# The order of one load queue in a two-block network: head pairs, gates and modulation weights

## The reference, cut to what matters

```python
proj = h @ w_in
(m_z, m_xbc, m_dt, b_qkv, c_qkv, c_f, d_q, d_kv, gate_logits) = jnp.split(proj, SPLIT_POINTS, axis=-1)
y_a = mamba2_branch(m_z, m_xbc, m_dt, ...)
y_b = moba_attention(heads(bq, N_HEADS), heads(bk, N_HEADS), heads(bv, N_HEADS), ...)
y_c = forgetting_attention(heads(cq, N_HEADS), heads(ck, N_HEADS), heads(cv, N_HEADS), ...)
y_d = sliding_window_attention(heads(d_q, N_HEADS), ...)
branch_out = jnp.einsum('bsiw,iwd->bsid', branches, w_branch)
gates = jax.nn.sigmoid(gate_logits.reshape(bsz, s_len, N_BRANCHES, D_MODEL))
return jnp.sum(gates * branch_out, axis=2) @ w_out
```

## Time and profile before

| | us |
|---|---|
| median of 3 runs | 1218.05 |
| the three runs | 1218.87, 1216.9, 1218.05 |
| the profiled execution | 1222.76 |
| its span, from the first to the last record | 1221.0 |
| TensorE busy in it | 1169.3 (96%) |
| VectorE busy | 496.0 (41%) |
| ScalarE busy | 215.0 (18%) |
| GpSimd busy | 79.7 (7%) |
| mean granted TensorE clock | 0.977 |
| moved from memory | 158.11 MB, 130 GB/s over the span |

### The profile page before, as it was taken

One profiled execution on the slowest core, in us unless ns is written; L12 is line 12 of the kernel. 1 busy time (PEld: TensorE's weight loads), 2 busy tenths in 40 slices (PEclk: granted clock), 3 DMA queues, 4 the chain that ended last, 5 costly groups with the idle time before them and its releaser, 6 DMA issues.

```text
span 1221.0 us, 19636 instructions
## 1 busy us (share of the span) xinstructions
PE 1169.3 (96%) x8368; PEld 958.6 (79%) x8368; DVE 496.0 (41%) x1232; ACT 215.0 (18%) x545; POOL 79.7 (7%) x119
## 2 busy tenths in 40 slices
PE   6999999999999999999998998999999999999997
PEld 5888888878787677777776876878778787877886
DVE  3343333424431210000004494657666665766332
ACT  3121121203100100000003321212122121213101
POOL 1100000000022000000001011010101101010000
PEclk8999999999999899999998999999999998999999
DMA  7426446371556233535343403031221404051230
GB/s 265 135 93 242 176 169 249 121 296 41 185 147 233 112 132 119 189 121 190 121 173 120 161 18 139 27 131 53 105 95 62 156 5 153 19 208 53 86 122 35
DMA packets 50570, 160.48 MB, mean 131 GB/s; under 512 B 5394, under 2 KB 10418, under 8 KB 50484
## 3 DMA queue, kind: packets, MB, share of 16 engines
q1 hardware_dynamic: 49764, 158.12, 36.5%
q10 hardware_dynamic: 720, 1.11, 0.3%
HBM read 158.11 MB, written 1.10 MB: 130 GB/s over the span
## 4 chain that ended last, share of the span: by engine, by line
PE 91%; DMA 4%; DVE 4%; ACT 0%; issue 0%; SPq 0%; DVEq 0%
PE bank L377 38%; PE bank L677 21%; PE bank L586 8%; PE bank L831 3%; DMA slots<-in_w_rwkv 2%; PE bank L985 2%; PE bank L509 2%; PE bank L818 2%; DVE arena L1657 1%; PE bank L712 1%; DMA slots<-in_w_heads 1%; PE bank L656 1%; PE bank L445 1%; PE bank L780 1%; PE bank L389 1%; PE bank L690 1%
## 5 line engine op out<-in xcount | busy, mean ns | idle before, releaser
L377 PE MATMUL bank<-hT,slots 128*128 128x256 f32 x1760 | 390.4, 382 | 5.9 <-DMA slots<-in_w_heads 3.7
L377 PEld LDWEIGHTS bank<-hT,slots 128*128 128x128 f32 x1760 | 335.3, 191 | 59.5 <-issue 10.3
L677 PE MATMUL bank<-hT,slots 128*128 128x256 f32 x1152 | 284.3, 396 | 17.5 <-DMA slots<-in_w_rwkv 16.3
L677 PEld LDWEIGHTS bank<-hT,slots 128*128 128x128 f32 x1152 | 217.5, 195 | 51.0 <-DMA slots<-in_w_rwkv 17.1
L1657 DVE SCALAR_TENSOR_TENSOR arena<-padA,par,arena 128x256 f32<-128x256 f32 x232 | 109.6, 530 | 0.0
L586 PE MATMUL bank<-slots,arena 128*128 128x512 f32 x240 | 105.0, 592 | 0.0
L377 PE MATMUL bank<-arena,slots 128*128 128x256 f32 x432 | 94.6, 381 | 0.0
L377 PEld LDWEIGHTS bank<-arena,slots 128*128 128x128 f32 x432 | 82.7, 191 | 11.5
L586 PEld LDWEIGHTS bank<-slots,arena 128*128 128x128 f32 x240 | 45.6, 190 | 52.3 <-issue 51.7
L1550 DVE SCALAR_TENSOR_TENSOR arena<-arena,bank 128x256 f32<-128x256 f32 x22 | 9.3, 422 | 134.9 <-ACT arena L1121 134.9
L1462 DVE SCALAR_TENSOR_TENSOR adaA<-arena,sc,adaA 128x1024 f32<-128x1024 f32 x24 | 30.7, 1283 | 78.2 <-DMA arena<-in_ada_w 78.0
(11 more groups left out here) (306 smaller groups left out, 1156.1 us busy)
## 6 DMA issues: line engine op xcount, KB each, us to landing
slots<-in_w_rwkv SPq DMA_DIRECT2D x72, 512.0 KB, 4.6
slots<-in_w_heads SPq DMA_DIRECT2D x68, 512.0 KB, 8.1
slots<-in_w_gu SPq DMA_DIRECT2D x44, 512.0 KB, 4.4
arena<-in_ada_w SPq DMA_DIRECT2D x24, 512.0 KB, 4.4
slots<-in_w_down SPq DMA_DIRECT2D x22, 512.0 KB, 3.8
slots<-in_w_br SPq DMA_DIRECT2D x32, 256.0 KB, 2.6
slots<-in_w_out SPq DMA_DIRECT2D x16, 512.0 KB, 5.4
slots<-in_w_y SPq DMA_DIRECT2D x16, 512.0 KB, 4.4
```

What stands on the lines that cost most here:

```text
L377: end = e.matmul(psum, w[:, k * P:(k + 1) * P], rhs[:, k, :], start=k == 0, stop=k == kt - 1)
L677: end = e.matmul(proj(w, q), slot[w][:, k * P:(k + 1) * P], hT[:, k, :], start=k == 0, stop=k == KT - 1)
```

## The change

Only SyncE's stream is changed, in `sp_heads`. No transfer is added or taken away, no wait names another step, and the streams of the four other engines stay as they are, instruction by instruction. What changes is the order of the requests within a pair i:

1. The nine head slices of pair i + 1 are asked for in the middle of pair i, behind gates 0 to 2 and modulation pieces 0 and 1, where before they stood at the start of pair i + 1, behind piece 5 of pair i.
2. The decay loads of pair i + 1 are asked for behind gate 4 of pair i, where before they stood behind slice CQ of pair i + 1.
3. Modulation pieces 0 and 1 stand behind gate 2 instead of gate 3, piece 2 stands ahead of gate 5, piece 3 ahead of gate 6; behind gate 7 only pieces 4 and 5 are left, where it was 3, 4 and 5.

```diff
+            def head_loads(i):
+                for n, before, step in ((BQ, "bc0", "qb"), (BK, "bc1", "kb"), (CQ, "dk0", "qc"), (CK, "dk1", "kc"), (DQ, "dv", "qd"),
+                                        (BV, "bc2", "vbc"), (CV, "bc3", "vbc"), (XS, None, "xs"), (ZS, None, "zs")):
                     if i:
-                        e.wait_ge(*dve.upto(f"mx.c11.{i - 1}"))
-                        e.wait_ge(*dve.upto(f"d11.{i - 1}"))
-                    else:
+                        e.wait_ge(*pe.upto(f"{step}.{i - 1}"))
+                    elif before:
+                        e.wait_ge(*pe.upto(before))
+                    load(e, n, a["w_heads"][i * NW + SLICE[n], :, :], f"w{n}.{i}")
...
+            if i == 0:
+                head_loads(0)
-            for j in range(4):
+            for j in range(3):
                 gate_load(j)
-            for n in range(3):
+            for n in range(2):
                 ada_load(n)
-            for j in range(4, 8):
-                gate_load(j)
-            for n in range(3, 6):
-                ada_load(n)
+            if i < PAIRS - 1:
+                head_loads(i + 1)
+            gate_load(3)
+            gate_load(4)
+            if i < PAIRS - 1:
+                e.wait_ge(*dve.upto(f"mx.c11.{i}"))
+                e.wait_ge(*dve.upto(f"d11.{i}"))
+                decay_loads(i + 1)
+            ada_load(2)
+            gate_load(5)
+            ada_load(3)
+            gate_load(6)
+            gate_load(7)
+            ada_load(4)
+            ada_load(5)
```

More of the change, by code:

```diff
@@ L2045, in ada_load @@
                 e.dma_start(adaW[n % 2], a["ada_w"][i * 6 + n, :, :]).then_inc(*in_ada[n % 2].step(f"ada{n}.{i}"))
[L2047 to L2054, removed]
-                    if i:
-                        e.wait_ge(*dve.upto(f"mx.c11.{i - 1}"))
-                        e.wait_ge(*dve.upto(f"d11.{i - 1}"))
-                    else:
+            def head_loads(i):
+                for n, before, step in ((BQ, "bc0", "qb"), (BK, "bc1", "kb"), (CQ, "dk0", "qc"), (CK, "dk1", "kc"), (DQ, "dv", "qd"),
+                                        (BV, "bc2", "vbc"), (CV, "bc3", "vbc"), (XS, None, "xs"), (ZS, None, "zs")):
+                    if i:
+                        e.wait_ge(*pe.upto(f"{step}.{i - 1}"))
+                    elif before:
+                        e.wait_ge(*pe.upto(before))
+                    load(e, n, a["w_heads"][i * NW + SLICE[n], :, :], f"w{n}.{i}")
+                    if i == 0 and n == CQ:
                         e.wait_ge(*dve.upto("cumT"))
@@ L2061, in sp_heads, with decay_loads @@
                         e.wait_ge(*to_cum.upto("cum"))
-                    e.dma_start(cm, bass.AP(cum_dram, (NH + 2 * i) * 3 * P, [[0, P], [3 * P, 2], [1, 3 * P]])).then_inc(*in_cm.step(f"cm.{i}"))
-                    e.dma_start(acb, bass.AP(cum_dram, 2 * i * 3 * P + P, [[0, P], [3 * P, 2], [1, T]])).then_inc(*in_acb.step(f"acb.{i}"))
-            for j in range(4):
+                        decay_loads(0)
+            def decay_loads(i):
+                e.dma_start(cm, bass.AP(cum_dram, (NH + 2 * i) * 3 * P, [[0, P], [3 * P, 2], [1, 3 * P]])).then_inc(*in_cm.step(f"cm.{i}"))
+                e.dma_start(acb, bass.AP(cum_dram, 2 * i * 3 * P + P, [[0, P], [3 * P, 2], [1, T]])).then_inc(*in_acb.step(f"acb.{i}"))
+            if i == 0:
+                head_loads(0)
+            for j in range(3):
                 gate_load(j)
-            for n in range(3):
+            for n in range(2):
                 ada_load(n)
-            for j in range(4, 8):
-                gate_load(j)
-            for n in range(3, 6):
-                ada_load(n)
+            if i < PAIRS - 1:
[13 more added lines that the diff above has]
+            ada_load(5)
         def sp_mix(e):
```

## The result

| | before | after |
|---|---|---|
| median of the timed runs, us | 1218.87 (7 runs, 1216.9 to 1225.69) | 1210.3 (7 runs, 1209.29 to 1212.22) |
| ratio after / before, 95% interval | | 0.9918 (0.9896 to 0.9941) |
| span of the profiled execution, us | 1221.0 | 1208.6 |
| start of BQ of pair 0 to start of L394, us | 279.45 | 271.93 |
| L394 to the first product with `w_br`, us | 2.85 | 1.80 |

What follows compares the result with a forecast made beforehand. TensorE, busy 96% of the span, was taken as the bound, losing time to waits and low clock. Terms summed to 8.6 us; less 3.3 for one slow transfer, 5.3 off 1218.05 gave 1212.7, range 1208.4 to 1215.9.

Steps and rivals of the forecast that it cites:

- What ends the stalls: Pair boundaries and L394: head slices no longer queue behind modulation pieces, and ada(5) ends before gate 7; 3.73 and 1.48 us.
- Gate 5, gate 7 and the decay loads: Inside the pairs: they land in time in the new request order, gate 5 having 9.6 us; cost 0.
- that contention: Around 170 us: GpSimd's moved mask additions could hold VectorE's modulation pieces by their own length, leaving the sum the same.
- The sum against the profiled execution: Whole traced execution: 3.73 + 1.69 + 1.48 + 1.7 = 8.6 us, from 1222.76 to 1214.2.
- The boundaries: Ahead of pairs 1 to 3: stalls of 3.73 us go, with 1.69 us of low clock; together 5.42 us.
- the last pair: Ahead of L394: TensorE waits for gate 7 on ScalarE alone, starting at about 329.47 instead of 330.95; 1.48 us saved.
- The clock behind L394: Around the L394 wait: the low clock goes once the stall is about 0.5 us; 1.7 us.
- Without that accident this boundary is worth 0.7, not 3.98: Ahead of pair 3: one slow transfer held not to be in ordinary runs, so 3.3 us come off the sum.
- rival B: Ahead of pair 3: the slow transfer is ordinary, so timed runs gain 8.6 us, to 1209.4; chance 0.22.

Runs made afterwards that it cites:

- only the slices: Against the kernel before, only head slices and decay loads move to the middle of the pair, modulation pieces stay; 1214.87 us against 1222.24, ratio 0.9939.

## Why the prediction was right, and where it was off

**What ends the stalls** was right, step by step. Ahead of BQ the head slices are in, and TensorE goes on without a break; pieces 4 and 5 are asked for at once; ada(5) is done before gate 7; L394 waits for ScalarE alone, 0.57 us against 0.5 forecast. Gate 5, gate 7 and the decay loads cost nothing, as costed, though gate 5 had not the queue to itself: the decay loads and piece 2 were in flight, and it took 4.9 us, not the 3.4 of a slice alone. The three additions of GpSimd that moved never fell on a VectorE instruction: in pair 1 they ran from 168.31 to 169.72 and ada(2) began at 170.23. What the Trainium skill says of that contention (SBUF — State Buffer, section "Who interferes with whom") was not put to the test.

**The sum against the profiled execution**, 8.6 us, was right and slightly low. From BQ of pair 0 to the first product with `w_br` the trace lost 282.30 - 273.73 = 8.57 us, and the products themselves 56.08 - 55.42 = 0.66 more, in all 9.2. By terms: the interval up to L394 was forecast to lose 3.73 + 1.69 + 1.48 = 6.90 and lost 7.52. The boundaries gave 0.76 more than forecast, the last pair 0.14 less. Pair 0 took 120.32 - 51.50 = 68.82 us before and 67.77 after, 1.05 less, where 0.78 was shown as idle; each of the three stalls was 0.2 to 0.3 us dearer than its row. Part of that is the drawing: idle time counts from the end of a matmul drawn 379 ns long, while the next could start about 0.22 us after its start, which makes 0.16. The rest, about 0.1 a stall, is open. The clock behind L394 was forecast at 1.7, and came to 1.05 + 0.66 = 1.71.

**The step that failed** is the one between the trace and the median: "Without that accident this boundary is worth 0.7, not 3.98". The profiled execution stood 4.7 us above the median of three, and I looked for that excess in the stall ahead of pair 3, called it an accident and took 3.3 us off. Three more executions with the order of before at that place had it, at 2.23, 2.70 and 2.44 us, each with the low clock behind it. It belonged to the kernel, so the forecast should have been the plain sum, rival B at 1209.4; the whole change measured 1210.3, 8.6 us under before, and in a second series 1210.56, 9.8 us under. The 4.7 us were scatter: 40 timed runs of before lie between 1214.05 and 1225.69 with a median of 1220.7. The three known to me happened to lie low, and the profiled execution stood 2.0 us above this median. So the medians of before and the traces do not tie an excess to a place; a second trace would have. The change measured lay inside the range only because the range had been drawn to reach B.

**The clock** was read rightly at the places where it fell, but the trace of one execution made it look surer than it is ahead of L394. There the idle time was 1.95, 2.02, 2.25 and 2.28 us in four executions; the clock fell behind the first two and not behind the other two. The 1.7 us there came two times in four, and what decides between them the traces do not show; a whole 1.7 was too sure a term, and it was luck that the trace before had it. The whole span shrank by 12.4 us, 3.2 more than the terms. That lies in the RWKV part, which the change does not touch: its waits for weights were 2.3 us shorter (16.3 to 14.0), and the clock fell behind four of the six instead of five. In the second trace of the whole change they were 15.1 us, with three falls.

**The parts** turned out not to be additive. The forecast gave the boundaries to the move of the slices and the last pair's end to the pieces. Either part alone ends the boundary stalls, and the pieces alone end the last pair's wait too.

## What to carry to other kernels

Where one engine asks for all loads in a fixed order and waits for their buffers, a wait on one stream holds up every other stream behind it; put the requests in the order in which their buffers come free and their data is needed, and look for the chain "transfer, use, next transfer" ahead of a late load before moving the load itself. When a single profiled execution is slower than the median, do not assign the difference to the most conspicuous row: profile once more first. A cause found in one queue is worth looking for in the other loops of the same program; here the unchanged RWKV loop held more than twice the gain of the change.

## What the runs showed of the hardware

- Idle time of TensorE and the granted clock behind it. Behind the 15 idle times at pair boundaries or ahead of L394 that were up to 1.18 us long the clock stayed at 1.00 each time; behind 1.95 to 2.28 us it fell to 1.2 GHz (0.50 from 332 to 334 us in the trace of before) in three cases of five; behind 2.29, 2.44 and 2.70 it fell each time. A fall cost 1.7 us. The length alone does not decide it: of the 54 waits for RWKV weights in the nine traces with the old order there, 2.2 to 4.1 us long, 39 had the low clock behind them (twelve matmuls in over 4 us) and 15 had not (in 2.86), among these one of 3.50 and one of 3.70. Before and the whole change again:

```profile
750.47 4.46 PE L677 MATMUL bank<-hT,slots 128*128 128x256 f32 x12 [4.13 <-DMA slots<-in_w_rwkv]
```

```profile
742.03 2.86 PE L677 MATMUL bank<-hT,slots 128*128 128x256 f32 x12 [3.70 <-DMA slots<-in_w_rwkv]
```

- One and the same request, piece 3 at the end of pair 2, took 5.7 to 6.1 us in all four executions with the order of before at that place, whatever memory it read, and 6.2 in "only the slices", against 4.3 to 4.6 at the other pair ends in the traces of before. Why is open.
- 512 KB copies from memory to memory landed 1.7 us apart in a row of twelve (eleven in 18.9 us).
